# First block of a two-block model: mixers in pieces between the chunks of both projections

## The reference

```python
xn = rms_norm(x, norm1_g)
h = xn @ w_in                      # 2048 -> 6176 columns
qa, ka, va, gdf, gdb, ra, qd, kd, vd = split(h)
oa = gla_mixer(qa, ka, va, gdf, gdb, ra, ...)   # gated linear attention, 4 heads, forward and backward
od = dilated_mixer(qd, kd, vd, q_norm_g, k_norm_g, positions)  # 12 heads of 128, rms norm and rotation of q, k
x = x + concat(oa, od) @ w_out     # 2048 -> 2048
x = x + peer_ffn(rms_norm(x, norm2_g), ...)     # experts, gathered rows
```

## Time and profile before

| | us |
|---|---|
| median of 3 runs | 2393.49 |
| profiled execution, its own time | 2404.86 |
| its span, first to last instruction | 2403.1 |
| TensorE busy | 2088.4 |
| VectorE busy | 1323.1 |
| ScalarE busy | 788.5 |

### The profile page before, as it was taken

The page is one execution under the profiler, slowest core; times in us unless marked ns, Lnnn a source line. Parts: engine busy times, 40 slices in busy tenths (PEclk is TensorE's granted clock), DMA queues, the critical chain, the costliest instruction groups (busy, mean ns, idle before and its releaser), DMA issues. The chain is left out here.

```text
span 2403.1 us, 21652 instructions
## 1 busy us (share of the span) xinstructions
PE 2088.4 (87%) x8141; PEld 1358.3 (57%) x8141; DVE 1323.1 (55%) x1944; ACT 788.5 (33%) x1600; POOL 263.1 (11%) x267
## 2 busy tenths in 40 slices
PE   6999967998898989977777898899777899999986
PEld 5888746884344444432223344444322798999875
DVE  4456537544555555645566555456544756565545
ACT  5344326322222122212222321222122555355334
POOL 0000000001112211112122111121211000000000
PEclk9999958999999999999999999999999899999988
DMA  6666601729999999999999999999998655466632
GB/s 212 194 193 193 197 4 44 263 83 396 427 427 428 427 428 428 425 428 412 429 409 423 428 427 428 427 428 425 413 428 363 213 162 164 138 205 196 187 127 83
DMA packets 87242, 727.80 MB, mean 303 GB/s; under 512 B 10177, under 2 KB 10305, under 8 KB 51681
## 3 DMA queue, kind: packets, MB, share of 16 engines
q0 software_dynamic: 36864, 536.89, 52.7%
q1 hardware_dynamic: 50272, 189.53, 24.5%
HBM read 722.18 MB, written 4.19 MB: 302 GB/s over the span
## 5 line engine op out<-in xcount | busy, mean ns | idle before, releaser
L1209 PE MATMUL bank<-ring,work 128*128 128x512 f32 x2048 | 964.6, 615 | 206.3 <-ACT work L1287 203.7
L1442 DVE CUSTOM_DVE_ANT_0 ring<-ring,mix_t 128x2048 f32<-128x2048 f32 x256 | 586.9, 2293 | 554.3 <-DMA ring<-in_peer_rows_dram,work 552.6
L1209 PEld LDWEIGHTS bank<-ring,work 128*128 128x128 f32 x2048 | 375.4, 193 | 727.5 <-issue 380.6
L481 DVE TENSOR_TENSOR ring_r<-ring,ring_r 128x1024 fp32r<-128x1024 f32 (+2 forms) x300 | 332.8, 1145 | 278.2 <-ACT ring_r L460 277.7
L1350 POOL DMA_INDIRECT ring<-in_peer_rows_dram,work x256 | 259.0, 1012 | 1287.1 <-PE bank L1209 964.9
L514 PE MATMUL bank<-ring_r,mix_r 128*128 128x512 f32 (+1 forms) x1248 | 394.2, 387 | 0.0
L1283 ACT ACTIVATE work<-work 128x1 f32<-128x1 f32 x256 | 51.9, 203 | 962.8 <-DVE work L1442 962.8
L460 ACT ACTIVATE ring_r<-ring 128x1024 fp32r<-128x1024 f32 (+2 forms) x300 | 288.6, 992 | 205.1 <-DMA ring<-in_w_out_dram 57.7
L514 PE MATMUL bank<-ring_r,act_r 128*128 128x512 f32 (+1 forms) x864 | 311.2, 391 | 9.2 <-DVE ring_r L481 9.2
L514 PEld LDWEIGHTS bank<-ring_r,mix_r 128*128 128x128 f32 x1248 | 234.3, 189 | 43.8
L511 PE MATMUL bank<-mix_r,ring_r 128*128 128x256 f32 (+1 forms) x1216 | 230.2, 292 | 12.0 <-DVE ring_r L481 12.0
(11 more groups left out here) (352 smaller groups left out, 1204.7 us busy)
## 6 DMA issues: line engine op xcount, KB each, us to landing
ring<-in_w_out_dram SPq DMA_DIRECT2D x64, 512.0 KB, 3.6
ring<-in_w_in_qk_dram SPq DMA_DIRECT2D x48, 512.0 KB, 3.6
ring<-in_w_in_rest_dram SPq DMA_DIRECT2D x48, 512.0 KB, 3.6
ring<-in_w_in_mo_dram SPq DMA_DIRECT2D x48, 384.0 KB, 3.4
h<-in_w_query_dram SPq DMA_DIRECT2D x8, 2048.0 KB, 11.0
ring<-in_w_in_ml_oz_dram SPq DMA_DIRECT2D x24, 512.0 KB, 3.6
h<-in_xa_wkv_dram SPq DMA_DIRECT2D x4, 2048.0 KB, 21.7
ring<-in_w_in_lru_dram SPq DMA_DIRECT2D x16, 512.0 KB, 3.7
```

The source lines that it names most:

```text
L481: dve.tensor_tensor(low(c), raw(c), plain(high(c)), ALU.subtract).then_inc(k.weights_low, 1)
L1209: m = pe.matmul(B[c][:, :], diag[:, d % 2, :], slots[:, d % DEPTH, 1, c * 512:(c + 1) * 512], start=first, stop=last)
L1442: dve.tensor_tensor_reduce(row, row, xn[:, t, :], 1.0, 0.0, ALU.mult, ALU.add, dots[:, p, j:j + 1]) \
```

## The change

Stages 2 to 6 become one program, `first_block`, of one stream of 130 chunks: gates, three blocks for the recurrence, nine blocks for attention in the order q, k, v for four heads at a time, and the output projection in pairs of blocks. Ticks 0 to 48 are the input projection, 49 to 64 the output projection. Chunks use banks 0 to 3 (the last two output blocks 4 to 7), pieces use banks 4 to 7. The recurrence has pieces at ticks 2 to 21; norm and rotation of eight heads at a time at ticks 17, 21, 29, 33, 41 and 45, the squares now on ScalarE; turning at 22, 23, 34, 35, 46, 47; the heads begin at ticks 24 to 51 and each ends three ticks later. Scores of all heads share one bank. Outputs of the mixers are split into high and low parts by the pieces themselves. The scratch memory of the recurrence lies over x, which is loaded a second time at tick 48. The experts' query weights and the two arrays come at ticks 56 to 60.

```diff
-        normalise(k, "norm1", k.x3, k.c("norm1_g"), k.act3, load=load_x, upcoming=in1)
-        beside = Beside()
-        rotate_beside(k, beside, in1.out(qk_job, qk_job.blocks - 1), in1.at(rest_job, 0) // PER_TICK)
-        project(k, in1, "in1", split_act, upcoming=out1, beside=beside)
-        gla(k)
-        dilated_turn(k)
-        attend(k, "dilated", DIL_H, ...)
-        k.recycle()
-        project(k, out1, "out1", split_mix, beside=beside, junk=junk)
+        query_in, keys_in, gain_in = first_block(k, split_act, from_act, residual)
...
+DIL_G = 4
+QK_TICKS = (17, 21, 29, 33, 41, 45)
+DIL_TURN = (22, 23, 34, 35, 46, 47)
+DIL_TICKS = (24, 26, 28, 30, 36, 38, 40, 42, 48, 49, 50, 51)
...
+def gla_beside(k, mem, beside, gates_in, qk_in, v_in, r_in, name="gla"):
+    def tensor(pe):
+        yield 2
+        pe.wait_ge(arrived, 48)
+        pe.wait_ge(*gates_in)
+        for t in range(NT):
+            pe.matmul(B[4 + t][:, :], gd_t[:, t * P:(t + 1) * P], up, start=True, stop=True).then_inc(logits, 1)
+        yield 4
+        pe.wait_ge(la_ready, 1)
...
+        for e in range(2):
+            yield 14 + e
...
+        for t in range(NT):
+            yield 19 + t
+            pe.wait_ge(y_done, t + 1)
...
+    def scalar(act):
+        yield 2
+        act.wait_ge(sized, 1)
+        act.activation(grow[:, :, :], tmp[:, :, :], ACT.Exp, scale=-1.0).then_inc(exped, 1)
+        act.wait_ge(exped, 1)
+        act.activation(tmp[:, :, :], grow[:, :, :], ACT.Ln, bias=1.0).then_inc(logged, 1)
...
+    def vector(dve):
+        yield 2
...
+        yield 3
+        dve.wait_ge(logged, 1)
+        dve.scalar_tensor_tensor(la[:, :, :], la[:, :, :], 0.0, tmp[:, :, :], ALU.min, ALU.subtract).then_inc(la_ready, 1)
...
+def rotate_beside(k, mem, beside, blocks_in, name="rotate"):
+    def scalar(act):
+        for n, tick in enumerate(QK_TICKS):
+            yield tick
+            act.wait_ge(*blocks_in[n])
+            for i in range(QK_HEADS):
+                act.activation(mem.qk_junk[:, i, :], ..., ACT.Square, accum_out=ss[:, n, i:i + 1]).then_inc(squared, 1)
+            act.wait_ge(meaned, n + 1)
+            act.activation(sd[:, n, :], rs[:, n, :], ACT.Sqrt).then_inc(rooted, 1)
+    def vector(dve):
+        for n, tick in enumerate(QK_TICKS):
+            yield tick
+            dve.wait_ge(squared, QK_HEADS * (n + 1))
+            dve.tensor_scalar(rs[:, n, :], ss[:, n, :], 1.0 / HD, EPS, ALU.mult, ALU.add).then_inc(meaned, 1)
+            yield tick + 1
+            dve.wait_ge(rooted, n + 1)
+            step(dve.reciprocal(rs[:, n, :], sd[:, n, :]))
+            for i in range(QK_HEADS):
+                m = dve.scalar_tensor_tensor(a, a, rs[:, n, i:i + 1], gains[:, n % 2, :], ALU.mult, ALU.mult)
...
+def dilated_beside(k, mem, beside, rotated, v_in, gla_low, in_ended, name="dilated"):
+    def tensor_scores(pe):
+        for h, tick in enumerate(DIL_TICKS):
+            yield tick
+            if h % DIL_G == 0:
+                pe.wait_ge(qk_taken, 4 * (h // DIL_G + 1))
+            if h >= 1:
+                pe.wait_ge(biased, h)
...
+    def vector_split(dve):
+        for g in range(GROUPS - 1):
+            yield 49 + g
+            dve.wait_ge(high, g + 1)
...
+    beside.tensor += [tensor_mix, tensor_turn, tensor_turn_qk, tensor_scores]
+    beside.vector += [vector_store, vector_divide, vector_split, vector_score]
+    beside.scalar += [scalar_split, scalar_high, scalar_take, scalar_take_qk, scalar_exp]
...
+def first_block(k, split_act, from_act, residual):
+    order = [c for job in (gates, gla, dil) for c in job.in_order()] + out1.in_pairs()
+    stream = Stream(k, order, banks=range(4), late_banks={(id(out1), 2): (4, 5), (id(out1), 3): (6, 7)})
...
+    def load(sp):
+        yield 48
+        sp.wait_ge(rotated, QK_BLOCKS)
+        sp.wait_ge(gla_turned, NT)
+        sp.dma_start(k.x3, ins["x"].rearrange("(t p) d -> p t d", p=P)).then_inc(x_back, 16)
+        yield 56
+        sp.wait_ge(stored, DIL_H)
+        load_query(sp, k, 0, query_in)
+        yield 58
+        sp.dma_start(shaped(k.h[:, 8192:10240], 2 * PEER_H, PEER_K), ins["sub_keys"]).then_inc(keys_in, 16)
+        yield 59
+        sp.dma_start(k.h[:, 10240:12288], ins["norm2_row"]).then_inc(gain_in, 16)
+        yield 60
+        load_query(sp, k, 1, query_in)
...
+    for s, need in ((0, (gla_low, NT)), (2, (low, 1)), (4, (low, 2)), (6, (stored, DIL_H - 2)), (7, (stored, DIL_H))):
+        stream.chunks[stream.at(out1, 0, s)].needs = [need]
+    out1.add_waits = [(x_back, 16)]
```

More of the change, by code:

```diff
@@ L627, in gla @@
+def gla_beside(k, mem, beside, gates_in, qk_in, v_in, r_in, name="gla"):
+    ins, B = k.ins, dict(zip(range(4, 8), k.banks[4:8]))
+    h3, gd_t, up, bias, out_g = mem.h3, mem.gd_t, mem.up, mem.bias, mem.out_g
+    la, tmp, grow, k_end, keep, q_t, k_t = mem.la, mem.tmp, mem.grow, mem.k_end, mem.keep, mem.q_t, mem.k_t
+    state, decay, stats = mem.state, mem.decay, mem.stats
+    q_in, k_in, y = grow, la, tmp
     S = lambda n: k.sem(f"{name}_{n}")
-    arrived, cleared = S("arrived"), S("cleared")
@@ L646, in inc_at @@
         i = sum(1 for m in range(n) if ((m % 3) if m < 6 else 3 - m % 3) % 2 == odd)
[L647 to L673, removed]
@@ new lines, in inc_at, with pool @@
+        return ((4, 5), (6, 7))[odd][i // 4], i % 4 * P
+    def load(sp):
+        yield 0
+        sp.dma_start(up, ins["gla_up"]).then_inc(arrived, 16)
+        sp.dma_start(bias, ins["gla_rows"][:, 0:512]).then_inc(arrived, 16)
+        sp.dma_start(out_g, ins["gla_rows"][:, 512:1024]).then_inc(arrived, 16)
+    def pool(eng):
+        yield 0
+        eng.memset(keep[:, :, :, :], 0.0).then_inc(cleared, 1)
+    def tensor(pe):
[7 more added lines that the diff above has]
+        for t in range(NT):
+            pe.matmul(B[4 + t][:, 0:256], k.c("tri_f"), la[:, t, 0:256], start=True, stop=True)
+            pe.matmul(B[4 + t][:, 256:512], k.c("tri_b"), la[:, t, 256:512], start=True, stop=True).then_inc(sums, 1)
+        for t in range(NT):
+            pe.matmul(B[6 + t][:, :], k.c("same"), la[:, t, :], start=True, stop=True).then_inc(tails, 1)
+        yield 5
+        pe.wait_ge(tails_out, 2)
+        for d in range(2):
+            for r in range(2):
+                for t in range(NT):
+                    m = pe.matmul(B[6][:, (d * 2 + r) * 4 + 2 * t:(d * 2 + r) * 4 + 2 * t + 2],
+                                  la[:, t, d * 256 + r * P:d * 256 + (r + 1) * P], k.c("half"), start=True, stop=True)
+        m.then_inc(tails, 1)
+        yield 8
+        pe.wait_ge(q_done, 2)
+        pe.wait_ge(k_done, 2)
+        pe.wait_ge(dec_done, 1)
+        for bank, src, turned in ((4, q_in, q_turned), (6, k_in, k_turned)):
@@ L676, in _ @@
                     for t in range(NT):
[L677 to L692, removed]
@@ L706, in _ @@
[L706 to L715, removed]
@@ L716, in _ @@
-            pe.wait_ge(kept, 4)
-            pe.wait_ge(states, 1)
+                        m = pe.transpose(B[bank + d][:, r * T + t * P:r * T + (t + 1) * P],
+                                         src[:, t, d * 256 + r * P:d * 256 + (r + 1) * P], k.c("ident"))
+                m.then_inc(turned, 1)
+        for d in range(2):
+            yield 10 + d
+            if d == 0:
+                pe.wait_ge(q_out, 2)
+                pe.wait_ge(k_out, 2)
             for e in range(2):
@@ L721, in _ @@
                     for r in range(2):
-                        hh = 2 * r + e
-                        for d in range(2):
[L724 to L732, removed]
@@ new lines, in tensor @@
+                        m = pe.matmul(B[4 + 2 * d + e][:, (t * 2 + r) * P:(t * 2 + r + 1) * P],
+                                      k_t[rows, d, r, t * P:(t + 1) * P], q_t[rows, d, r, t * P:(t + 1) * P],
+                                      start=True, stop=True)
+                m.then_inc(scores, 1)
+        yield 12
+        pe.wait_ge(kept, 4)
+        pe.wait_ge(ke_done, 2)
+        pe.wait_ge(*v_in)
+        for d in range(2):
+            for r in range(2):
+                for s in range(3):
+                    c = s if d == 0 else 3 - s
+                    for e in range(2):
+                        hh = 2 * r + e
+                        rows = slice(64 * (c % 2), 64 * (c % 2) + 64)
+                        bank, col = inc_at(d, r, s)
+                        m = pe.matmul(B[bank][64 * e:64 * e + 64, col:col + P],
+                                      k_end[rows, c // 2, d * 256 + hh * 64:d * 256 + hh * 64 + 64],
+                                      h3[rows, c // 2, H_VA + hh * P:H_VA + (hh + 1) * P], start=True, stop=True)
@@ new lines, in tensor @@
+        m.then_inc(incs, 1)
+        for e in range(2):
+            yield 14 + e
+            if e == 0:
+                pe.wait_ge(states, 1)
+            rows = slice(64 * e, 64 * e + 64)
+            for t in range(NT):
+                for r in range(2):
+                    hh = 2 * r + e
+                    for d in range(2):
```

(10 more changed lines are left out.)

608 lines of the change are left out of this document (338 added, 270 removed).

## The result

The changed kernel takes 2353.38 us (median of 4 runs, 2351.52 to 2356.08) against 2392.64 us of the kernel before: ratio 0.9833, 95% interval [0.9809, 0.9856]. A second set on one chip gave 2353.61 us (5 runs) against 2398.25 us (23 runs), ratio 0.9825 [0.9804, 0.9845]. The change is worth 39 to 45 us by these two sets; 58.4 us had been forecast. The time of 2353.4 us lies 0.6 us inside the upper end of the range of 2325 to 2354 us. The profiled execution took 2356.08 us with a span of 2354.3 us.

The account below looks back on a forecast made before the run. TensorE was taken as the bound in both projections, idling 38.8 of the 116.3 us between; 2404.86 - 118.9 + 55.5 + 5 = 2346.5 us profiled, the 58.4 us difference carried to the median: 2335 us, range 2325 to 2354.

Parts of the forecast that it names:

- rival A: The forecast itself: TensorE keeps streaming through the merged stage; 2335 us, own range 2327 to 2345; chance 0.64.
- What comes back on TensorE, 55.5 us: Matmuls of recurrence (24.4 us), turning (5.1) and attention (26.0), now between chunks, priced start-to-start at full clock.
- the gates: Two chunks of the first projection, taken at 8.3 us, with their start at half clock staying.
- The waits, 5 us: TensorE's waits for pieces of other engines: 2, 1.5 and 0.5 us at three places, 1 for the rest; bounds 1.9 and 25.
- tick 2 to 4: Recurrence, gate logits to log-decay: 12.6 us of work against 12.6 available, a wait of 0 to 3 us, taken as 2.
- the rotation on VectorE between the halves of y: Tick 18 to 20, y of the recurrence: the rotation's 4.3 us on VectorE makes TensorE wait 1.5 us.
- rival C: Clock falls in ticks 14 and 15 under 4.9 us of small tiles each; 2345 us; chance 0.11.
- The step from one profile to the median: Runs' median lay 11.4 us below the profiled execution; the 58.4 us difference was carried over unchanged, 2393.5 to 2335 us.
- Queries, keys, the second copy of x: Loads moved to ticks 48 and 56 to 60: cost nothing, at most 3 us for the last 2 MB.
- rival E: x or queries come late and hold the additions or DMA-bound expert part, up to 8 us: 2343 us; chance 0.05.
- Rival D: Slower: VectorE's in-order queue loses the lead for good, deciding from 0.98 us waiting per tick; 2408 us at 1.2; chance 0.04.
- Rival B: Waits at tick borders, 0.2 to 0.6 us more per tick, 10 to 35 us: 2345 to 2370, centre 2352; chance 0.16.

## Why the prediction was right or wrong, point by point

- **The mechanism** (rival A: TensorE keeps streaming) was right. TensorE is busy for 98% of the stage, and doubling a TensorE piece costs its full price, while adding a VectorE piece costs 2 to 3.5 us for 8.2 us of work. The chunks and pieces together held to 4 us.
- **What comes back on TensorE, 55.5 us**: right in sum, within some 4 us. The transposes of a head cost 0.43 us as assumed. The state products had been taken at the middle between 1.4 and 2.9 us, 2.2, and took 1.5 (104.64 to 106.16 us); the scores of the recurrence took 3.3 instead of 2.8 us, so these errors cancel in part. With 5.9 us for the gates (25.85 to the logits at 37.21 us, less two chunks), 348.2 for the chunks and 55.5 for the pieces the stage would be 409.6 us. It was 424.2: 8.4 of waits, 2.7 of clock after the longest, and 3.5 over. Of these, about 0.05 us per piece is seen in the timeline of a head, and of 420 groups of three chunk matmuls 100 started 0.69 or 0.70 us apart and not 0.68, some 1.2 us; the rest stays open. The gates were forecast at 8.3 us, as before, and took 5.9, because the clock was at 1.00 from 26.5 us on in this execution (0.50 from 27 to 30 us in the profile before, 0.69 from 26.5 to 32 us in the second profile of after). These 2.4 us are luck of one profile, and they hide as much of the other terms' error in the 7 us by which the stage ended late.
- **The waits, 5 us**: the term was mis-sized. The places were partly right: tick 2 to 4, for which I had taken 2 us, shows no wait at all; the wait before the first group's turning was in the tick I named, 0.7 us in place of 0.5, and the two later groups, which I had not counted, brought 0.9 us each. The large one was not where I put it. I counted the rotation on VectorE between the halves of y; the late piece was ScalarE's eight squares in front of the weight splits (shown by moving them). I had summed ScalarE's work per tick and not asked what stands behind it in the queue just after a block's wait has used up its lead. What the wait does to the clock, 2.7 us more (1.7 in the second profile), was not in the sum; I had it only for the small tiles of rival C.
- **Rival C** did not occur. (Its premise, a fall of the clock under small tiles, is in the first profile of before, but not in the second.) In ticks 14 and 15 the clock is 1.00 in the changed kernel, with the same small tiles that ran at 0.50 in the earlier trace rows:

```profile
117.10:122.00 4.90, 4.90 (x43) 3.73 (x41) 3.41 (x4) 3.69 (x4) 0.00 (x0) 1.00 0.41 129
127.50:132.40 4.90, 4.90 (x42) 3.69 (x40) 1.39 (x2) 2.11 (x2) 0.00 (x0) 1.00 0.39 132
```

- **The step from one profile to the median** failed, and it is the largest error. I carried 58.4 us from the profiled execution to the median and argued that the 11.4 us between them lay in the DMA-bound part. Of it, 7.2 us can lie in the very stage that is removed: an execution whose recurrence ran at full clock has 7.2 us less to give back. The forecast saving less these 7.2 and less the stage's 7 us of lateness is 44.2; the second set measured 44.6, the kernels without experts 43.3. That this comes out so well is no proof: it takes for granted that the median execution of before has its recurrence at full clock, and three of the four profiles of that program, one of them the median execution without experts, have it at 0.50. In that pair the first block alone gave 48.8 us, and 4.5 came back behind it. So the recurrence's level is shown as a cause of 7 us between executions; how much of the gap between 51 us in the first profiles and 39 to 45 in the medians it makes up, and what the rest is, stays open. The 39.3 us of the first set rest on four runs of before; the 23 runs of the second set span 2390.5 to 2401.7 us, so four can easily lie 5 us off.
- **Queries, keys, the second copy of x**: as forecast, nothing. TensorE waits for none of them, and the expert part (1360 to 1366 us in two profiles, 1360 to 1362 before) is not longer by the 8 us of rival E. The 2 MB loads landed in 8.6 us in the median against 8.1.
- **Rival D** was far away. The waits come to 8.4 us in 65 ticks, 0.13 us per tick against the 0.98 at which it would have decided.
- **Rival B** happened in small: its mechanism gave 3 us more than forecast, and 6 with the clock, and not 10 to 35.
- **The time** of 2353.4 us lies inside the range, but where rival B had its times (2345 to 2370, centre 2352), while B's mechanism gave only 6 us. Of the 18 us above A's 2335, 7 are the stage that ended late, 2.5 came behind the first block in the profiled execution (1901.9 us from norm2 to the end against 1899.3), and 8.7 are the step to the median: the profiled execution of after lies 2.7 us above its median, where I had carried 11.4. A's own range of 2327 to 2345 us was missed by 8 us. That the range held is more luck than judgement.

## What to carry to other kernels

When stages are merged into one stream, add up the bound engine's start-to-start times: that part of the forecast held to some 4 us of 410. For the rest, don't add up work per tick, but go to each place where an in-order engine has just lost its lead to a wait and read what stands there in front of the next weight split; small work there cost 5 us here, and one number in a table of ticks moved it. A stage that runs alone with gaps and small tiles had either clock here from one execution to the next, so take its length from more than one profile before you call it the gain.

## What the runs showed of the hardware that I had not expected

The granted clock of the same unchanged stretch of the kernel before was 0.50 in three profiles and 1.00 in one (341 to 345 us; 20, 20, 21 and 34 matmuls), with TensorE busy throughout in all four. TensorE's busy time before it differed little: in all four it was 9.8 to 10.3 of the 17 us from 320 to 337 us. The granted clock of these 17 us was 0.80 in the one and 0.70 in the three. Between dense chunks the same tiles had 1.00 (115 to 134 us) in all eight profiles of the changed kernel and its variants. The Trainium skill (TensorE: Matmul & The Clock Gate, section "Part 1: The HAM clock gate") calls the moment of the change run-variable by some matmuls at a kernel's start. Here the level lasted for the rest of the recurrence's products and was worth 6.3 us. A wait of 4.1 to 4.2 us inside the dense stream was followed by half clock in all five profiles that have it, from 158.5 to nearly 164 us in the first profile of the changed kernel and for some 3.5 us in the second (2.7 and 1.7 us lost), while the waits of 0.9 and 1.4 us left the windows at 1.00.
